# Attention heads in pairs: two heads' scores and two heads' outputs back to back on the matrix engine

## The reference, cut to what matters

```python
def mixer_ab(h, ...):                      # layer 0: attention "a"
    q, k, v = split_qkv(h, qk_g)
    att = windowed_attention(q, k, v, sink, rel_table)   # softmax(q k^T/8 + bias, sink) v
    gb, gc, u = jnp.split(h[..., QKV_COLS:], 3, axis=-1)
    conv = gb * short_conv(gc * u, conv_w, conv_b)
    return jnp.concatenate([att, conv], axis=-1)

def mixer_cd(h, ...):                      # layer 1: attention "c"
    q, k, v = split_qkv(h, qk_g)
    att = blocked_dense_attention(axial_rope(q), axial_rope(k), v)   # softmax(q k^T/8) v
    u = short_conv(h[..., QKV_COLS:], conv_w, conv_b)
    x0, x1, vh = jnp.split(u, 3, axis=-1)
    kfull = hyena_filter(h.shape[1], ...)
    z = x1 * vh
    y = x0 * (fft_long_conv(z, kfull) + skip * z)
    return jnp.concatenate([att, y], axis=-1)
```

## Time and profile before

| what | value |
|---|---|
| three timed runs | 1495.74, 1497.18, 1497.48 us; median 1497.18 |
| the profiled execution | 1500.95 us, of which the span from the first to the last instruction is 1499.0 |
| TensorE matmul busy | 1436.5 us, 96% of the span |
| VectorE, ScalarE busy | 1092.0 us (73%), 699.0 us (47%) |
| chain that ended last | TensorE has 90% of it, VectorE 5% |
| attention "a", from its first scores to the start of `wout0` | 271.8 to 323.1 us |
| attention "c", from its first scores to the start of `wout1` | 801.4 to 857.9 us |
| mean granted TensorE clock | 0.980 of full |

### The profile page before, as it was taken

How to read it: one execution, slowest core, us unless ns; L and a number is a source line. 1 busy time by engine, 2 the same in 40 slices (tenths; PEclk the granted TensorE clock), 3 DMA queues, 4 the chain that set the end, 5 groups by cost and what they waited for, 6 DMA issues and landing times.

```text
span 1499.0 us, 26571 instructions
## 1 busy us (share of the span) xinstructions
PE 1436.5 (96%) x11012; PEld 1353.3 (90%) x11012; DVE 1092.0 (73%) x1831; ACT 699.0 (47%) x1125; POOL 24.8 (2%) x24
## 2 busy tenths in 40 slices
PE   3999999999999999999999999999999899899998
PEld 3999998889999999999988699999996669799998
DVE  6788898777777879878667766565683676586776
ACT  3333536444434354344464343434564765555543
POOL 0000000000000000000000000000010030000000
PEclk9999999899999999999999999999996899999999
DMA  9996957236777568567533046565322204345552
GB/s 393 387 386 247 364 211 276 87 133 269 289 284 305 195 261 329 230 243 303 217 127 113 29 169 239 211 227 182 141 85 99 104 23 145 123 169 189 192 177 77
DMA packets 32183, 308.25 MB, mean 206 GB/s; under 512 B 3480, under 2 KB 5784, under 8 KB 7360
## 3 DMA queue, kind: packets, MB, share of 16 engines
q1 hardware_dynamic: 32064, 306.56, 53.0%
HBM read 305.48 MB, written 1.06 MB: 205 GB/s over the span
## 4 chain that ended last, share of the span: by engine, by line
PE 90%; DVE 5%; ACT 2%; issue 1%; DMA 1%; SPq 0%; DVEq 0%; ACTq 0%
PE bank L833 14%; PE bank L658 13%; PE bank L662 13%; PE bank L659 13%; PE bank L750 7%; PE bank L752 7%; PE bank L757 6%; PE bank L628 3%; DMA X<-in_x 1%; PE bank L903 1%; PE bank L619 1%; PE bank L676 1%; PE bank L914 1%; DVE WL L1776 1%; PE bank L734 1%
## 5 line engine op out<-in xcount | busy, mean ns | idle before, releaser
L1776 DVE TENSOR_TENSOR WL<-ring,WH 128x1024 fp32r<-128x1024 f32 x418 | 500.2, 1222 | 46.1 <-ACT WH L1235 43.8
L1235 ACT ACTIVATE WH<-ring 128x1024 fp32r<-128x1024 f32 x418 | 427.8, 1054 | 126.9 <-PE bank L833 55.3
L658 PE MATMUL bank<-XH,WH 128*128 128x256 f32 x1680 | 409.3, 282 | 1.4 <-ACT WH L1235 1.4
L659 PE MATMUL bank<-XL,WH 128*128 128x256 f32 x1680 | 407.7, 281 | 0.0
L658 PEld LDWEIGHTS bank<-XH,WH 128*128 128x128 f32 x1680 | 316.2, 188 | 7.1 <-issue 5.5
L659 PEld LDWEIGHTS bank<-XL,WH 128*128 128x128 f32 x1680 | 316.2, 188 | 0.5 <-issue 0.5
L662 PE MATMUL bank<-XH,WL 128*128 128x256 f32 x1680 | 233.8, 282 | 1.0 <-DVE WL L1776 1.0
L662 PEld LDWEIGHTS bank<-XH,WL 128*128 128x128 f32 x1680 | 213.9, 188 | 1.2 <-DVE WL L1776 1.2
L1315 ACT ACTIVATE SG<-bank 128x256 f32<-128x256 f32 x88 | 33.8, 384 | 376.2 <-PE bank L662 358.7
L750 PE MATMUL bank<-GH,WH 128*128 128x256 f32 x840 | 202.5, 279 | 0.7 <-ACT WH L1235 0.7
L752 PE MATMUL bank<-GL,WH 128*128 128x256 f32 x840 | 202.4, 279 | 0.0
(11 more groups left out here) (318 smaller groups left out, 1656.4 us busy)
## 6 DMA issues: line engine op xcount, KB each, us to landing
ring<-in_stream SPq DMA_DIRECT2D x132, 1536.0 KB, 6.6
scr<-in_stream SPq DMA_DIRECT2D x15, 1536.0 KB, 9.9
PR<-in_stream SPq DMA_DIRECT2D x15, 1536.0 KB, 8.5
att<-in_stream SPq DMA_DIRECT2D x15, 1536.0 KB, 10.4
ring<-in_stream SPq DMA_DIRECT2D x9, 1024.0 KB, 5.0
ring<-in_stream SPq DMA_DIRECT2D x10, 512.0 KB, 3.6
kf_mix<-in_stream SPq DMA_DIRECT2D x2, 1536.0 KB, 15.9
con<-in_consts SPq DMA_DIRECT2D x1, 2000.0 KB, 17.0
```

Source lines behind the costliest of these rows:

```text
L658: pe.matmul(o, part(WH, u, k), XH[:, k, :], start=(k == 0), stop=False)
L659: pe.matmul(o, part(WH, u, k), XL[:, k, :], start=False, stop=False)
L1235: act.activation(part_all(WH, u), raw(u), ACT.Copy).then_inc(*mark("high", u))
L1776: dve.tensor_tensor(part_all(WL, u), raw(u), part_all(WH, u).bitcast(F32), ALU.subtract)\
```

## The change

The two attentions named in `PAIRED` go through their heads two at a time, on all three engines. On TensorE a pair is: transposes of h, scores of h+2 and of h+3, transposes of h+1, first fill, outputs of h and of h+1, second fill. The same units lie in the same order, with two fills in a pair; in "c" `z_spectrum` takes the first fill of the pairs 2 and 4, and `convolve` both fills of the last pair. ScalarE evicts both heads' transposes before the exponentials of the next two heads; VectorE does the maxima of both next heads, then (in "a") a split, then both `probs`. In the diff the parts for TensorE, ScalarE and VectorE follow in this order.

```diff
+    PAIRED = ("a", "c")
...
-                ahead = len(A.get("score_banks", (4, 5)))
-                for h in range(ahead):
-                    scores(h)
-                lead()
-                for h in range(n):
+                def turn(h):
                     take(turn_bank(a, h), "turned", a, h)
                     pe.wait_ge(*at("probs", a, h))
...
                     last.then_inc(*mark("probs_turned", a, h))
+
+                ahead = len(A.get("score_banks", (4, 5)))
+                for h in range(ahead):
+                    scores(h)
+                lead()
+                if a in PAIRED:
+                    for h in range(0, n, 2):
+                        turn(h)
+                        if h + 2 < n:
+                            scores(h + 2)
+                            scores(h + 3)
+                        turn(h + 1)
+                        fill(h, 0)
+                        attend(h)
+                        attend(h + 1)
+                        fill(h, 1)
+                    return
+                for h in range(n):
+                    turn(h)
                     fill(h, 0)
                     if h + ahead < n:
                         scores(h + ahead)
...
                 def fill(h, k):
-                    if k == 1:
-                        unit("win0", passes, 10 + h)
+                    unit("win0", passes, 10 + h + k)
...
                 def fill(h, k):
-                    units = {0: 14, 1: 15, 3: 16, 5: 17}
-                    if h in units and k == 1:
-                        unit("win1", passes, units[h])
-                    if h == 1 and k == 1:
+                    units = {(0, 0): 14, (0, 1): 15, (2, 1): 16, (4, 1): 17}
+                    if (h, k) in units:
+                        unit("win1", passes, units[h, k])
+                    if (h, k) == (0, 1):
                         z_transposes()
-                    if h in (2, 4) and k == 2:
+                    if h in (2, 4) and k == 0:
                         z_spectrum(h // 2 - 1)
-                    if h >= 6 and k < 2:
-                        convolve(2 * (h - 6) + k)
+                    if h == 6:
+                        convolve(2 * k)
+                        convolve(2 * k + 1)
...
+                if a in PAIRED:
+                    exps(0)
+                    exps(1)
+                    for h in range(0, n, 2):
+                        turned(h)
+                        between(h)
+                        turned(h + 1)
+                        if h + 2 < n:
+                            exps(h + 2)
+                            exps(h + 3)
+                        between(h + 1)
+                        leave(h + 1)
+                    return
...
+                if a in PAIRED:
+                    probs(0)
+                    probs(1)
+                    for h in range(0, n, 2):
+                        if h > 0:
+                            low(h // 2 - 1)
+                        between(h)
+                        if h + 2 < n:
+                            maxima(h + 2)
+                            maxima(h + 3)
+                        after(h)
+                        if h + 2 < n:
+                            probs(h + 2)
+                            probs(h + 3)
+                        between(h + 1)
+                        after(h + 1)
+                    low(n // 2 - 1)
+                    return
...
-                    def with_head(h):
-                        conv_unit(9 + h)
-                        split_to(u0 + 8 + h + PARTS)
-
-                    attention("a", with_head)
+                    attention("a", lambda h: conv_unit(9 + h), after=lambda h: split_to(u0 + 8 + h + PARTS))
```

More of the change, by code:

```diff
@@ L1528, in leave, with turned @@
                         act.activation(o, att_out(a, c), ACT.Copy).then_inc(*mark("mixed", a, c))
+                def turned(h):
+                    act.wait_ge(*at("probs_turned", a, h))
+                    if h >= 2:
+                        act.wait_ge(*at("attended", a, h - 2))
+                    act.activation(pt[:, h % 2, :, :], bank[turn_bank(a, h)].rearrange("p (u q) -> p u q", u=2), ACT.Copy)\
+                        .then_inc(*mark("turned", a, h))
+                if a in PAIRED:
[11 more added lines that the diff above has]
+                    return
                 for h in range(ahead - 1):
```

## The result

Four timed runs of the changed kernel took 1468.49 to 1474.27 us, median 1471.38; four runs of the kernel before took 1488.48 to 1497.48, median 1496.46. The ratio of the two is 0.986, with a 95% interval from 0.9823 to 0.9897, so the change is worth 15 to 26 us. The profiled execution has a span of 1466.5 us, where that of before had 1499.0.

A forecast was written before the change was run, and what follows sets the result against it. The prediction took TensorE to bound both attentions, with VectorE next in "a". Savings of 6.8 us in "a" and 7.9 in "c" made 14.7, and 1497.18 - 14.7 gave 1482.5 us, range 1480 to 1489.

The forecast's parts named there:

- Scores and outputs pair in the middle of the loop as they do at its ends: In both attentions, a second head's scores or outputs come free on TensorE; 12.4 us, or 0 without overlap.
- The block that leaves least slack: VectorE's work in "a" before head 6: `probs(6)` done at 307.4, wanted at 308.2, 0.8 us of slack.
- the fall behind the first head: In "a", the clock at 0.57 of full from 277.56 to 285.00 us was expected to stay.
- the wait of 0.6 for `spectra_mult(1)`: In the last pair of "c", TensorE was to wait 0.6 us for VectorE after the transposes of head 7.
- the new waits of "c": TensorE's added waits in attention "c": 1.55 us together, possibly 0 or some 4.
- One sign: In the changed profile, "c" from its first scores to `wout1` was to take 48.6 us.
- 1.0, 4.65 and 0.55: Savings in us in "c": head 0 to head 2, head 2 to head 6, and head 6 to `wout1`.
- the 1.7 that lie behind the start of `wout1`: Saving of 1.7 us in `wout1`: TensorE's 1.73 wait for a convolution output from VectorE was to go.
- The timed runs have their median 3.8 below it, so the forecast is 1497.18 - 14.7: For the whole kernel, the timed level before less the summed saving gives 1482.5 us.
- VectorE did not become the bound: Rival: VectorE late per pair, TensorE waiting about 4 us in "a", 1 to 3 in "c"; 1487 to 1490; chance 0.12.
- Outputs overlap as scores do: Rival in both attentions: only the scores pair, outputs sharing all rows do not; 6 x 1.01 comes back, 1488.5; chance 0.03.
- No stretch of low clock came in behind the new waits: Rival: clock falls at pair boundaries, 3.2 us each, five eating the gain; 1498.5, six 1501.7; chance 0.03.

The follow-up runs named there:

- e14: The kernel before with the one-column `q_stats` matmuls of the third layer made 128 columns wide; median 1487.42 us, 0.9962 of before.
- e13: The changed kernel with the one-column `q_stats` matmuls of the third layer made 128 columns wide; median 1471.16 us.
- e1: The kernel before, unedited, timed against itself; median 1493.98 us, ratio 0.9993.
- e11: The kernel before with 7 more warm-up matmuls behind `wout1`; median 1488.13 us.
- e12: The kernel before with 11 more warm-up matmuls behind `wout1`; median 1495.18 us.
- e16: The kernel before with 8 more warm-up matmuls inside the feed-forward block ahead of the third layer; median 1489.18 us.
- e8: The changed kernel with only attention "c" in pairs, "a" as before the change; median 1476.34 us, 0.9886 of before.
- e9: The changed kernel with 4 more warm-up matmuls behind `wout1`; median 1474.63 us.
- e10: The changed kernel with 8 more warm-up matmuls behind `wout1`; median 1474.15 us.
- e15: The changed kernel with 4 more warm-up matmuls inside the feed-forward block ahead of the third layer; median 1479.92 us.
- e4: The changed kernel with 87 more warm-up matmuls behind `wout1`, so the third layer starts about as late as before; median 1487.66 us.

## Why the prediction was wrong

**The edited stretches: right.** The step "Scores and outputs pair in the middle of the loop as they do at its ends" holds in all pairs. With no low clock in either, "a" went from 48.3 to 41.9, 6.4 us (forecast 6.8); "c" gained 7.1 (e14 against e13), and the start of `wout1` 1.9, 9.0 together (forecast 7.9). The sum of 14.7 was 15.5, with errors of -0.4, +0.9 and +0.2 that partly cancel. Details differ. VectorE was 0.46 and 0.30 us late for heads 6 and 7 of "a", where 0.1 was expected for head 7 alone. The block that leaves least slack was named, but its 0.8 us of slack was worked out with the fall behind the first head in TensorE's time. That fall was absent: TensorE was ready for head 6 at 27.3 us behind its first transposes, where 30.6 had been laid out, and VectorE at 27.6, where 29.8 had. And the wait of 0.6 for `spectra_mult(1)` in "c" did not come, since VectorE was done within 0.2 us of the transposes of head 7; the new waits of "c" came to some 1.1 us in place of 1.55. One sign is met by luck: "c" from its first scores to the start of `wout1` was to take 48.6 us and took 48.36. The prediction's own terms for that stretch are 1.0, 4.65 and 0.55, which from 56.4 gives 50.2; the 48.6 also takes off the 1.7 that lie behind the start of `wout1`. Of the 8.05 us that the profiled "c" lost, about 1.7 are a shorter fall (3.4 us at the lower clock in place of 6.8).

**The step that failed: "The timed runs have their median 3.8 below it, so the forecast is 1497.18 - 14.7".** It took the level of the kernel before from three runs that agreed within 1.7 us, and took it as constant outside the edited stretches. The 106 later runs have a median of 1492.9 and lie in two groups 10.7 us apart. The three came from the upper group, 4.3 us above the common median and 9.1 above the median of the lower group. From the lower group's 1488.1, the same sum gives 1473.4; the ten runs of the changed kernel, nine of them with a clock of 0.990 or more, have a median of 1471.75.

**The price of the clock had the wrong place.** The forecast had the fall behind the first head of "a" as something that stays. It is absent in all profiles of a paired "a", but also in five of the seven profiles of an unpaired one (e1, e11, e12, e14, e16; present in that of before and in e8), so this says little. It had no term at all for the third layer, which held 35 us at a clock of 0.56 in the profile of before and whose row I had not read, since nothing was edited there. The range ended at 1480; a missing fall in an attention, 3.2 us, was put below it with a chance of 0.05. The sum of the miss of 11.1: 9.1 for the level (1497.18 in place of 1488.1), 1.6 for the change (16.3 between e14 and e13 in place of 14.7), and 0.4 left. This takes the changed kernel's runs as free of the long fall, which nine of ten are if the line of 0.988 is right for them; if it isn't, some of the 9.1 lies elsewhere.

**How much the change is worth.** By the edited stages it is 15.5 us. With wide `q_stats` in both kernels the medians are 16.3 us apart; against the sampled kernel before it is 21, and the rest is how often each has the fall. By the line of 0.988 that share was 54 of 106 before and 1 of 10 after. e9, e10 and e15 show that the changed kernel isn't free of it (8 of their 18 runs are under 0.988), so part of the difference is luck of the sample, and part can be the line itself, above which the changed kernel stays with a fall of 13.7 us. Whether anything is left for the edit stays open. All kernels with "c" fully paired have 11 such runs of 50, all others with the narrow matmuls 108 of 196, but the line favours the first, and 12 of the 50 are e4. No run here shows what in the pairs of "c" could reach a layer that begins 225 us later.

**The rivals.** VectorE did not become the bound (two waits, 0.76 us). Outputs overlap as scores do. No stretch of low clock came in behind the new waits in the profiles of the changed kernel.

## What to carry to other kernels

Here two groups of matmuls that use opposite halves of the array cost as much as one when nothing else stands between them, so heads of 64 features are worth ordering by twos; look for a place where the kernel already does it and read the pitch there. Before a forecast in absolute microseconds, read the granted clock of every stage, the unedited ones too, and ask whether the few timed runs hold all that the kernel can do: three runs within 1.7 us said nothing about a second group 10 us below. If a stage falls to the lower clock by chance, take out what precedes the fall before measuring anything else: here widening some matmuls cost nothing and took the spread of 12 runs of the kernel before from 14 us (e1) to 5 (e14). And a line on the mean clock that separates one kernel's runs has to be drawn anew for another kernel, from its own profiles.

## What the runs showed of the hardware

The same program falls to the lower clock in the same stage in about half of its executions (54 of 106, by the mean clock): for 24 us in its first profile, for 14 in that of e1, and for 3.4 in that of its near copy e11. The two groups of runs are 10.7 us (0.7%) apart. The page "TensorE: Matmul & The Clock Gate" of the Trainium skill, Part 1, says that the clock's ramp at the start of a kernel varies from run to run and costs under 1% of a typical span; these runs agree in the size, though their fall lies in the middle of the kernel. What TensorE did ahead of the long falls was a row of one-column matmuls, 16 records at a pitch of 0.11 us; 128 columns wide they took no longer than 1.87 us to the next group, against 1.79, and none of 12 runs of the kernel before was in the slower group. Why narrow matmuls should do this isn't shown.

Matmuls in opposite halves of the array overlapped whole: four records of scores take 1.06 us to the next group and eight take 1.08; for outputs, which share all rows, it is 1.01 and 1.02.
